# A two-layer encoder trunk on one core: the router of the expert stage taken tile by tile, the first token tile ahead of the second

## The reference

```python
def _grouped_moe(x, w_router, b_router, w_gu, w_down):
    t = x.reshape(B * S, D)
    probs = softmax(t @ w_router)                        # 256 x 16
    sel = (probs + b_router).reshape(-1, 4, 4)
    group_score = top_k(sel, 2)[0].sum(-1)
    best_group = argmax(group_score)
    _, local = top_k(sel of the best group, 2)           # two experts of that group
    w = probs at the two, divided by their sum
    for e in range(16):
        g, u = split(t @ w_gu[e]); y = (silu(g) * u) @ w_down[e]
        out = out + gate[:, e:e + 1] * y
```

## Time and profile before

| | us |
|---|---|
| median of three executions (lowest, highest) | 689.04 (688.61, 690.35) |
| the profiled execution | 691.68 |
| its span, first to last instruction | 690.0 |
| TensorE matmul busy | 655.5 (95%) |
| VectorE busy | 284.3 (41%) |
| ScalarE busy | 139.7 (20%) |
| mean granted clock of TensorE, share of full | 0.984 |

### The profile page before, as it was taken

How to read it: one execution, slowest core, us unless ns; L and a number is a source line. 1 busy time by engine, 2 the same in 40 slices (tenths; PEclk the granted TensorE clock), 3 DMA queues, 4 the chain that set the end, 5 groups by cost and what they waited for, 6 DMA issues and landing times.

```text
span 690.0 us, 7113 instructions
## 1 busy us (share of the span) xinstructions
PE 655.5 (95%) x2746; PEld 292.3 (42%) x2746; DVE 284.3 (41%) x730; ACT 139.7 (20%) x321; POOL 22.6 (3%) x41
## 2 busy tenths in 40 slices
PE   5999999999999999999979998999999999999974
PEld 4854564465333333333324454546333333333321
DVE  0001303256535335253445344456553444435356
ACT  1003234021121121121222042312021121021212
POOL 2040100000000000000000011200000000000000
PEclk9999999998999999999999999999999999999998
DMA  8999903261999999999999980823899999999991
GB/s 318 388 405 348 425 17 134 110 237 58 417 421 422 420 421 422 422 421 421 419 417 414 421 337 9 359 101 144 326 423 422 420 421 420 423 419 423 419 389 64
DMA packets 41431, 231.43 MB, mean 335 GB/s; under 512 B 10153, under 2 KB 10153, under 8 KB 15794
## 3 DMA queue, kind: packets, MB, share of 16 engines
q1 hardware_dynamic: 36960, 230.72, 81.7%
q10 hardware_dynamic: 4434, 0.21, 0.4%
HBM read 229.87 MB, written 1.05 MB: 335 GB/s over the span
## 4 chain that ended last, share of the span: by engine, by line
PE 81%; DMA 9%; DVE 5%; ACT 2%; SPq 1%; POOL 1%; issue 1%; POOLq 0%; DVEq 0%; ACTq 0%
PE pb L635 28%; PE pb L435 16%; PE pb L662 14%; DMA ring<-in_w_down 8%; PE pb L487 4%; PE pb L682 3%; PE pb L789 2%; PE pb L613 2%; PE pb L391 1%; PE pb L615 1%; PE pb L398 1%; PE pb L409 1%; DMA h<-in_x 1%; PE pb L538 1%; PE pb L579 1%; POOL bufA L372 1%
## 5 line engine op out<-in xcount | busy, mean ns | idle before, releaser
L435 PE MATMUL pb<-ring,hT 128*128 128x512 f32 x320 | 141.7, 595 | 0.8 <-DVE hT L1619 0.8
L662 PE MATMUL pb<-ring,bufC 128*64 128x512 f32 x512 | 117.0, 597 | 4.9 <-DVE bufA L1433 2.7
L635 PE MATMUL pb<-ring,hT 128*64 128x512 f32 x512 | 114.6, 594 | 2.0 <-DMA ring<-in_w_gu 2.0
L635 PE MATMUL pb<-ring,bufB 128*64 128x512 f32 x512 | 113.2, 593 | 0.0
L1407 DVE STREAM_TRANSPOSE bufC<-bufC 32x128 f32<-32x128 f32 x256 | 102.9, 402 | 3.8
L1433 DVE COPY bufA<-pb 32x512 f32<-32x512 f32 x64 | 43.7, 682 | 122.9 <-PE pb L662 121.9
L435 PEld LDWEIGHTS pb<-ring,hT 128*128 128x128 f32 x320 | 59.3, 190 | 69.7 <-issue 67.7
L635 PEld LDWEIGHTS pb<-ring,hT 128*64 128x64 f32 x512 | 36.0, 137 | 75.0 <-issue 68.0
L635 PEld LDWEIGHTS pb<-ring,bufB 128*64 128x64 f32 x512 | 36.2, 137 | 71.8 <-issue 70.0
L662 PEld LDWEIGHTS pb<-ring,bufC 128*64 128x64 f32 x512 | 35.0, 136 | 72.7 <-issue 68.1
L1018 ACT ACTIVATE bufA<-pb 32x512 f32<-32x512 f32 x64 | 37.7, 589 | 115.9 <-PE pb L662 115.1
(11 more groups left out here) (230 smaller groups left out, 430.0 us busy)
## 6 DMA issues: line engine op xcount, KB each, us to landing
ring<-in_w_gu SPq DMA_DIRECT2D x128, 1024.0 KB, 23.3
ring<-in_w_down SPq DMA_DIRECT2D x64, 1024.0 KB, 25.5
ring<-in_w_in_a SPq DMA_DIRECT2D x12, 1024.0 KB, 17.9
ring<-in_w_out_a SPq DMA_DIRECT2D x4, 1024.0 KB, 21.0
ring<-in_w_q_b SPq DMA_DIRECT2D x4, 1024.0 KB, 22.6
ring<-in_w_out_b SPq DMA_DIRECT2D x4, 1024.0 KB, 23.4
ring<-in_w_kv_shared SPq DMA_DIRECT2D x2, 1024.0 KB, 29.0
h<-in_x SPq DMA_DIRECT2D x4, 256.0 KB, 5.0
```

The source lines that it names most:

```text
L435: last = mm(pb[bank][:, :], hT[:, k, t * P:(t + 1) * P], slot(i0 + k // 2)[0][:, k % 2, c * HALF:(c + 1) * HALF], start=k == 0, stop=k == ...
L635: last = mm(pb[0][c * 64:(c + 1) * 64, :].rearrange("p (a n) -> p a n", a=2), xe[m % 2][:, k, g * SLOTS:(g + 1) * SLOTS], slot(u_gu(l, u) ...
L662: last = mm(pb[2][c * 64:(c + 1) * 64, :], heT[u == EXPERTS - 1][:, (2 * hf + j) * 64:(2 * hf + j + 1) * 64], w[:, j, c * HALF:(c + 1) * H ...
```

## The change

Router, places, table and gathers are taken one tile at a time; tile 0 goes ahead.

- Transposes of tile 0's sum move into the first half of tile 1's products (k = 2), and there at k = 5 come the `w_sum` product and all eight `route_rows` of tile 0. In the second half, at k = 5, `place(l, 0)` counts tile 0's places, and at k = 7 the four transposes of tile 1's first half follow.
- `route(l, t)` chooses for one tile; `route(l, 0)` runs on VectorE before the statistics of tile 1, `places(l, 0)` makes tile 0's half of the table, and `pick_early` tells TensorE.
- Behind the products TensorE gathers both halves of tile 0 before it does the rows of tile 1; the two gathers of tile 1 stay last. ScalarE copies three of the four parts, VectorE one.
- ScalarE goes from exponential to square root and back once more in each layer (`warm`).
- The counts are copied to `raw` (the `counted` signal), and minimum and maximum are taken from that copy.

```diff
@@ tensor
             def route_rows(l, t, ks):
                 for k in ks:
-                    last = mm(pb[0][:, t * EXPERTS:(t + 1) * EXPERTS], hT[:, k, t * P:(t + 1) * P], w_norm[l][:, k, :],
+                    last = mm(pb[1 + t][:, 0:EXPERTS], hT[:, k, t * P:(t + 1) * P], w_norm[l][:, k, :],
                               start=k == 0, stop=k == KC - 1)
-                    if t == 0 and k == 0:
+                    if t and k == 0:
                         last.then_inc(freed, 1)
+            def place(l, t):
+                pe.wait_ge(chosen, 2 * l + t + 1)
+                mm(pb[1 + t][:, 16:32], tri[:, :], oh[:, t, :], start=True, stop=True)
+                mm(pb[1 + t][:, 32:48], ones[:, 0:1].to_broadcast([P, P]), oh[:, t, :], start=True, stop=True).then_inc(placed, 1)
...
-                return {1: first_tile, 6: sums}
+                def first_rows():
+                    pe.wait_ge(router_ready, l + 1)
+                    wait_hT(2 + 2 * l, 0)
+                    mm(pb[1][:, 64:96], ones[:, 0:1].to_broadcast([P, P]), w_sum[:, l, :, :].rearrange("p n e -> p (n e)"),
+                       start=True, stop=True)
+                    route_rows(l, 0, range(KC)).then_inc(logits, 1)
+                return {2: first_turns, 5: first_rows}, {5: lambda: place(l, 0), 7: lambda: turn_sum(l, 1, 0)}
...
-            project(U_WO, 1, 0, 2, mix_done)
-            project(U_WO, 1, 1, 3, mix_done, before_moe(0))
+            early, late = before_moe(0)
+            project(U_WO, 1, 0, 2, mix_done, early)
+            project(U_WO, 1, 1, 3, mix_done, late)
...
-                for f, bank in enumerate((3, 2, 1, 3)):
-                    gather(0, f, bank)
+                gather(0, 0, 0)
+                turn_sum(l, 1, 1)
+                gather(0, 2, 1)
+                pe.wait_ge(hT_dve, 3 + 2 * l)
+                route_rows(l, 1, range(0, 4))
+                wait_hT(2 + 2 * l, 1)
+                route_rows(l, 1, range(4, KC)).then_inc(logits, 1)
+                stay_awake(3, 2)
+                pe.wait_ge(ln_ready, 2 * (2 * NT * l + 1) + 1)
+                for c in range(2):
+                    seed(0, c)
+                stay_awake(3, 1)
+                place(l, 1)
+                pe.wait_ge(ln_ready, 2 * (2 * NT * l + 1) + 2)
+                seed(1, 0)
+                gather(0, 1, 3)
+                gather(0, 3, 2)
                 gate_up(0)
@@ scalar
+                take_hT(2 + 2 * l, 0, 0)
+                ln_std_part(2 * l, 0)
+                A(warm[:, 0:1], ones[:, 0:1], ACT.Exp)
+                exps_of(0)
+                A(warm[:, 1:2], ones[:, 0:1], ACT.Sqrt)
+                take_x(0, 0, 0)
+                take_hT(2 + 2 * l, 1, 0)
+                ln_std_part(2 * l, 1)
+                A(warm[:, 2:3], ones[:, 0:1], ACT.Exp)
                 take_x(0, 2, 1)
+                exps_of(1)
+                take_x(0, 1, 3)
@@ vector
+            def places(l, t):
+                dve.wait_ge(placed, 2 * l + t + 1)
+                if t == 0:
+                    V.tensor_copy(raw[t], pb[1 + t][:, 16:48])
+                link(V.tensor_tensor(r_a[:, t, :], pb[1 + t][:, 16:32], oh[:, t, :], ALU.mult))
+                if t == 0:
+                    make_pick(t).then_inc(pick_early, 1)
+                else:
+                    make_pick(t).then_inc(pick_ready, 1)
+                    V.tensor_copy(raw[t], pb[1 + t][:, 16:48]).then_inc(counted, 1)
...
                 ln_sum(n, 0, h, 0)
                 ln_tile(n, 0, h, (4, 5), (6, 7), turns + 2)
+                dve.wait_ge(logits, 2 * l + 1)
+                link(V.tensor_copy(bufC[:, 1440:1472], pb[1][:, 64:96]))
+                route(l, 0)
                 ln_half(n, 1, 0, h, 0)
-                dve.wait_ge(sums_done, l + 1)
-                V.tensor_copy(bufC[:, 1440:1472], pb[0][:, 32:64])
+                places(l, 0)
                 take_hT(2 + 2 * l, 1, 0)
                 ln_half(n, 1, 1, h, 0)
                 ln_tile(n, 1, h, (4, 5), (6, 7), turns + 4, False)
```

More of the change, by code:

```diff
@@ L150, in build @@
         d_old = st[:, 128:160]
+        raw = [bufC[:, 1472 + 32 * n:1504 + 32 * n] for n in range(NT)]
         near = st[:, 64:96].rearrange("p (e t) -> p e t", t=NT)
+        warm = sb("warm", [P, 8])
         dest = sb("dest", [P, QUADS, NT])
@@ L163, in build @@
         consts, counted = sem("consts"), sem("counted")
-        cols_in, router_ready, summed, x_dve, sums_done = (
-            sem("cols_in"), sem("router_ready"), sem("summed"), sem("x_dve"), sem("sums_done"))
+        cols_in, router_ready, summed, x_dve = (
+            sem("cols_in"), sem("router_ready"), sem("summed"), sem("x_dve"))
         turned = sem("turned")
@@ L456, in before_moe, with first_turns @@
             def before_moe(l):
-                def first_tile():
+                def first_turns():
                     for j in range(2):
                         turn_sum(l, 0, j)
-                def sums():
-                    turn_sum(l, 1, 0)
+                def first_rows():
                     pe.wait_ge(router_ready, l + 1)
                     wait_hT(2 + 2 * l, 0)
-                    mm(pb[0][:, 32:64], ones[:, 0:1].to_broadcast([P, P]), w_sum[:, l, :, :].rearrange("p n e -> p (n e)"),
-                       start=True, stop=True).then_inc(sums_done, 1)
-                return {1: first_tile, 6: sums}
+                    mm(pb[1][:, 64:96], ones[:, 0:1].to_broadcast([P, P]), w_sum[:, l, :, :].rearrange("p n e -> p (n e)"),
+                       start=True, stop=True)
+                    route_rows(l, 0, range(KC)).then_inc(logits, 1)
+                return {2: first_turns, 5: first_rows}, {5: lambda: place(l, 0), 7: lambda: turn_sum(l, 1, 0)}
             for first in (x_got, ov[0]["w_used"], ov[1]["w_used"], ov[0]["z"], ov[1]["z"]):
@@ L580, in seed @@
                        start=True, stop=False, skip_group_check=True)
[L582 to L593, removed]
                 Q0, E0 = QUADS * l + START, EXPERTS * l + START
@@ L599, in gather @@
                     half, t = f // 2, f % 2
-                    if f == 0:
+                    if m == 0 and f == 0:
+                        pe.wait_ge(pick_early, l + 1)
+                    elif f == (0 if m else 1):
                         pe.wait_ge(pick_ready, Q0 + (m + 1))
@@ L882, in _ @@
             pe.wait_ge(outT_sb, 4)
-            project(U_WOB, 1, 0, 2, mix_done)
-            project(U_WOB, 1, 1, 3, mix_done, before_moe(1))
+            early, late = before_moe(1)
+            project(U_WOB, 1, 0, 2, mix_done, early)
+            project(U_WOB, 1, 1, 3, mix_done, late)
             moe(1)
@@ L991, in _, with exps_of @@
             take_hT(1, 1, 0)
[L992 to L995, removed]
             def moe(l):
[L999 to L1003, removed]
+                def exps_of(t):
+                    act.wait_ge(rt_exp_in, 2 * l + t + 1)
+                    A(r_prob[:, t, :], r_logit[:, 0:EXPERTS], ACT.Exp, bias=r_s[:, 0:1], scale=-1.0,
+                      accum_out=r_s[:, 2:3]).then_inc(rt_exp, 1)
                 Q0, E0 = QUADS * l + START, EXPERTS * l + START
@@ L1119, in _ @@
                 exps(n)
[L1120 to L1123, removed]
             moe(1)
@@ L1434, in take_y @@
                                       pb[2][t * BLOCK:(t + 1) * BLOCK, :]).then_inc(y_sb[t], 1)
-                make_pick(0).then_inc(pick_ready, 1)
-                V.reduce_max(extra_f[:, 0:1], pb[1][:, 32:64], AX_X)
-                V.tensor_scalar(count, pb[1][:, 0:64], float(BLOCK), None, ALU.min).then_inc(counted, 1)
+                places(l, 1)
+                dve.wait_ge(counted, l + 1)
+                link(V.tensor_tensor(r_low[:, 0, :], raw[0][:, 16:32], raw[1][:, 16:32], ALU.max))
+                V.reduce_max(extra_f[:, 0:1], r_low[:, 0, :], AX_X)
+                V.tensor_scalar(count.rearrange("p (a t e) -> p t a e", a=2, t=NT),
+                                bufC[:, 1472:1536].rearrange("p (t a e) -> p t a e", a=2, t=NT), float(BLOCK), None, ALU.min)
                 link(V.tensor_scalar(pos[:, :, :].rearrange("p e t -> p t e"), r_a, 1.0, None, ALU.subtract))
-                take_x(l, 1, 2)
-                take_x(l, 3, 3)
                 weigh(l)
+                take_x(l, 3, 2)
                 if l == 0:
```

131 lines of the change are left out of this document (53 added, 78 removed).

## The result

| | before | after |
|---|---|---|
| median (us) | 689.37 (4 executions, 688.61 to 690.35) | 684.22 (4 executions, 682.24 to 684.65) |
| ratio, 95% interval | | 0.9919 (0.9895 to 0.9943) |
| profiled execution, its span | 691.68, 690.0 | 682.24, 680.5 |
| start of tile 1's products to the end of the last gather, layer 0 | 33.30 | 30.09 |
| the same, layer 1 | 33.49 | 30.10 |

The change gains 5.2 us, 0.8%; in a second series the ratio was 0.9924 (0.9910 to 0.9938). The forecast was 684.5.

A forecast was written before the change was run, and what follows sets the result against it. Each expert stage was taken to start with `gate_up(0)`, behind the chain to the last gather. 2.9 + 3.1 - 2 x 0.75 = 4.5 us off 689.04 gave 684.5; range 682.0 to 687.3.

The forecast's parts named there:

- The bound: Expert stage: stream and TensorE about even, both started by `gate_up(0)`; if it comes x us earlier, both move by x.
- rival (b): Expert stages: loads set the end and do not start with `gate_up(0)`, so nothing moves, 689.0; chance 0.06.
- The stretch: From start of tile 1's products to last gather's end: 30.4 us, 2.9 earlier in layer 0, 3.1 in layer 1.
- Products: Tile 1's products on TensorE, with tile 0's work put inside: 17.9 us, ending 2.0 later than now.
- Logits to choice of tile 1: Behind the products, from tile 1's logits to the end of its choice on VectorE: 4.4 us.
- The choice of one tile: On VectorE, choosing for one tile takes 3.3 us, where two tiles take 4.10.
- slack of tile 0's choice: Choice falls at about 146.3, TensorE asks at 147.8 in the products' second half: hidden with 1.5 us to spare.
- ScalarE's slack: ScalarE behind the products, before tile 1's exponential: free at 156.15, wanted at 156.4.
- rival (c): ScalarE before tile 1's exponential: table switch takes 2 x 1.28, exponential 1.0 us late per layer, 686.5; chance 0.03.
- The prediction's list in words: Gain in layer 0: logits 1.7 later, choice 0.8 shorter, places and table 0.2, two gathers 2.0 gone, low clock 1.0 gone.
- The clock: TensorE around rows, fillers and gathers: remaining clock falls cost 0.75 us a layer, half of layer 1's present 1.5.
- Rivals (d) and (e): (d) tile 0's choice over 1.5 us late, products stand, 688.5, chance 0.05; (e) thin rows lower clock in products, 692.8, 0.04.

The follow-up runs named there:

- the one of 868.52 us: Kernel before with one full product between tile 0's and tile 1's router rows: disturbed profiled execution, not read; median 691.79 against 689.40, ratio 1.0033.
- the two further schedules: Changed kernel, second early gather behind tile 1's rows, seed ahead of choice, one filler: 684.50; also four transposes behind products, copied by ScalarE: 683.42, again 683.77.
- the late load of one experiment: Changed kernel without the early load of the root's table, so it falls before tile 1's root: 686.38 against the kernel before's 688.92, ratio 0.9966.

## Why the prediction was right, point by point

**The bound.** Right. The distance from the last gather to the last landing stayed 185 to 186 us in both kernels and both layers (184.8 to 186.1 over all profiles but the one of 868.52 us), so rival (b), the stream that hides it, falls: the stage's end moves with its start, to within this 1.3 us. Gains below it, like those of the two further schedules, can't be followed through the stage. TensorE's waits for weights were 1.1 + 0.6 us in layer 0's stage, near.

**The stretch.** 30.4 us were summed, 30.09 measured. Products: 149.08 - 131.39 = 17.69 against 17.9. Behind them 12.40 against 12.5. Logits to choice of tile 1 4.36 against 4.4. The choice of one tile 3.24 against 3.3; slack of tile 0's choice 1.8 against 1.5; ScalarE's slack 0.49 against 0.25; the table load 1.28, so rival (c) falls. The Trainium skill ("ScalarE: Activation LUTs", What ACT_TABLE_LOAD costs) would have put a drain of about 1.4 us more on the tightest engine of the chain; the late load of one experiment shows that this would have been felt (0.72 us a layer for a shift of 1.28), and the profile shows that it is not there, since the next instruction begins 0.01 us behind the load.

The prediction's list in words doesn't add up to its own 2.9: -1.7 + 0.8 + 0.2 + 2.0 + 1.0 is 2.3. It leaves out that the way from the logits to the start of the choice became shorter, 2.0 to 1.15 us by its own times and 2.00 to 1.12 by the profiles, and it counts 0.2 for places and table that its times don't contain. The sum by times is the one that the 30.4 rests on, and it held.

**The clock.** This term was mis-sized, and in two ways that cancelled. I kept 0.75 us a layer for low stretches that would remain; in both profiles of the changed kernel none did. But I also took the profiled kernel before, with 2.5 us lost to the clock, for its usual execution. Two of its three profiles have that loss, and it is 2.9 us, since in layer 0 the fall also reached tile 1's rows (3.23 us instead of 2.75) and made the logits late: 1.34 us there, not 1.0. The third profile lost nothing on the path: 31.96 us in both layers. So the gain is 2 x (31.96 - 30.09) = 3.7 us of schedule and up to 2.9 us of clock (33.30 + 33.49 - 2 x 31.96), by the execution, and the medians, 4.8 and 5.2 us apart, lie between 3.7 and 6.6. That the two errors cancelled, and the median came within 0.3 us of the forecast, is luck.

How the 5 us of the medians divide between schedule and clock is not shown. The time of an execution goes with its mean granted clock: in the kernel before, the five executions at 0.982 average 690.8 us and the two at 0.991 average 685.1, and the median clock is 0.985 before and 0.992 after. At 0.990 four executions before average 685.9 us and three after 684.5, only 1.4 less. That isn't the schedule's share either, since a low stretch hidden under fillers lowers the mean clock and costs nothing.

**What the schedule's 3.7 us are.** The prediction listed them in one sum; the runs separate them. Early gathers 1.54 a layer, the split of the choice with all that it adds to the products 0.33. At full clock I had 1.9 in layer 0 and 1.6 in layer 1 for both together, measured 1.87. In the changed kernel tile 1's choice ends 26.37 us after the products' start and in the third profile before 26.27, so nothing is won up to the choice; all of the 1.87 lies behind it, where two gathers stand instead of four.

**Rivals (d) and (e)** did not happen, but were real. Pushing tile 0's rows 3.5 us later made both happen at once, and the kernel was then no faster than before. The slack that the change has there is 1.8 us.

**Forecast and span.** The profiled span fell by 9.5 us where 4.5 were written, and that is not the change alone: 2.21 us lie ahead of it, where the one profile had two clock falls that the other had not, up to 2.9 are the clock on the changed stretch, and 0.7 lie behind the gathers.

## What to carry to other kernels

Compare two profiles stretch by stretch from the first changed instruction on: the spans here differed by 9.5 us, the changed stretches by 6.6, the medians by 5. When a chain on one engine ends last, another engine's work that depends on the first half of the data can move ahead of it: here two gathers of 1.96 us brought 1.54, and splitting the chain itself a fifth of that. And a short idle time of TensorE amid full products can be dear, since the clock can fall behind it: in one profile 1.55 us of wait cost 3.5, in both layers.

## What the runs showed of the hardware that was not expected

The clock's falls differ between executions of one program. In the kernel before, layer 0's low stretch lay at 153 us for 6.8 us twice and at 155.7 us for 3.4 us once, with the price of 1.3 us or nothing; ahead of the change the same code ran low near 74 to 77 and 94 to 97 us in most profiles and not at all in one. Executions of the kernel before lie up to 7.3 us apart, 684.55 to 691.81, and the shorter ones have the higher mean clock (0.991 in the shortest, 0.986 in the longest). That the clock is all of this spread is not shown. The changed kernel had no idle time of TensorE over 0.1 us and no fall between products and gathers in its two profiles, and the usual two falls ahead of them in one.

TensorE lost the clock while the profile had it 100% busy, amid and behind products 16 columns wide. The Trainium skill ("TensorE: Matmul & The Clock Gate", Part 1) says that activity releases the throttle; in this trace the clock fell all the same while the profile had TensorE busy. Why a given execution falls and another doesn't was not tested, and stays open.
